# VectorE's w_ada chunks in halves around a linear chunk's two halves, in a two-block transformer kernel

## The chip, the cores and the metric

One NeuronCore of one Trainium2 chip runs the whole kernel. The metric is the device time of one execution in microseconds (us); the median of several runs counts. TensorE (PE in the profile) does the matrix products, VectorE (DVE) and ScalarE (ACT) work on elements, SyncE (SP) issues the DMA loads, GpSimd (POOL) does next to nothing here.

## The reference

Two blocks, batch 1, 256 tokens, width 2048, all in float32.

```
mod = silu(c) @ w_ada + b_ada                    # w_ada: 2048 x 12288; six parts of 2048
shift_a, scale_a, gate_a, shift_f, scale_f, gate_f = split(mod, 6)
h = rms_norm(x, g_attn_pre) * (1 + scale_a) + shift_a
proj = h @ w_in                                  # 5456 columns
mixed = concat(differential_attention(...), indexed_sparse_attention(...)) @ w_o
x = x + gate_a * rms_norm(mixed, g_attn_post)
h = rms_norm(x, g_ffn_pre) * (1 + scale_f) + shift_f
x = x + gate_f * rms_norm((silu(h @ w_gate) * (h @ w_up)) @ w_down, g_ffn_post)
x = second_block(x)                              # latent attention, a gated convolution; no w_ada
```

`silu(c) @ w_ada` is a vector times a matrix of 96 MB; the other products have 256 rows.

## The kernel before

**Chunks.** All weights pass through one ring of five slots (`raw`, `NRAW` = 5) of 1 MB: a chunk is 512 rows by up to 512 columns, held as 128 partitions by four row blocks. `chunk_plan` writes down the order of all chunks by hand in `PLAN`: linear chunks (`lin`) and, strewn between them, chunks of w_ada (`ada`, group g of 512 columns, quarter j of the rows). SyncE loads them in that order (`load_chunk`); the load of chunk c waits until chunk c - 5 has been used: for a w_ada chunk of VectorE's until `s_ada` has counted it, for a linear chunk until the wlo of its second half is written (`s_lo`).

**A linear chunk** is used in two halves (units) of two row blocks. ScalarE copies a half, rounded, to `whi` (L1046), VectorE writes the rest, `raw - whi`, to `wlo` (L1656), and TensorE makes twelve matmuls of it: activations hi times whi, hi times wlo, lo times whi (L579 to L581), for two blocks of 128 tokens. There are three slots of whi and wlo (`NHL`): whi of unit i waits for the matmuls of unit i - 3.

**A w_ada chunk** is used in one of two ways. The 32 chunks of groups 0 to 7 are done by TensorE (L533), all before 180 us. The other 64 (groups 8 to 23) are VectorE's: `ada_step` adds four row blocks, each scaled by an element of silu(c), to two accumulators (L1636, L1639), in turn even and odd; after quarter 3 it adds the two (L1648, `s_sum`). TensorE then sums over the partitions (`ada_take`, L514, L515 or L519), and VectorE's `mod` adds the bias or multiplies G by it (L1618, L1620) and frees the bank.

**The order of each engine's queue.** Every engine walks the same plan with a `Walk`. `UNITS` lists the halves of linear chunks and, as one entry each, the w_ada chunks, in the plan's order; `LIN` lists the linear halves alone. Before the matmuls of linear unit u, `chunk` calls `split_to`, which issues all that stands in `UNITS` up to linear unit u + 2 (`AHEAD` = 2). After the unit it calls `tick`, which lets each of up to three lanes of side work (attention heads in lane 0 and 1, the turning of operands) issue one step. So VectorE's queue is: the w_ada chunks that stand ahead of a linear chunk in the plan, wlo of its first half, a step of the lanes, wlo of its second half, a step of the lanes.

Between 176 us and 545 us (the last columns of w_in's first part, the rest of w_in, w_o) the plan has about one w_ada chunk of VectorE's ahead of each linear chunk, 48 in all, and two ahead of it at four places (before the w_in chunks that VectorE reaches at 206 and 315 us, and the first two chunks of w_o at 402 and 418 us). In the feed-forward part it has one ahead of every second linear chunk, 16 in all, until 880 us.

**When a group's sum is taken.** `split_to` notes in `sum_at` the linear unit at which the last quarter was issued; `can_take` lets the sum be taken two units later. It is taken by the lane of differential attention at fixed steps of it or, where lane 1 is empty, by `idle` at the next tick.

**G.** The gains of the post norm lie in `G`. The load of g_ffn_post into it (L2490) stands in SyncE's queue right behind the load of the chunk four places after the first one of w_gate's third column group; `mod` of group 20 multiplies G, in a tick at the end of w_up's second column group, ahead of the multiplies of `gt` (L2155) that end this w_up.

Of the kernel before, what the change touches and what calls it, by code (L numbers as in the profile page):

```python
# [46 lines left out]
ADA_ON_PE = (4, 0, 5, 1, 6, 2, 7, 3)  # L47
# [90 lines left out]

PLAN = chunk_plan()

UNITS = [(c, h) for c, item in enumerate(PLAN) for h in range(2 if item[0] == "lin" else 1)]
LIN = [u for u in UNITS if PLAN[u[0]][0] == "lin"]
LIN_NO = {u: i for i, u in enumerate(LIN)}
UNIT_AT = {u: i for i, u in enumerate(UNITS)}

ADA_NO = {c: i for i, c in enumerate(c for c, item in enumerate(PLAN) if item[0] == "ada" and item[1] not in ADA_ON_PE)}


def unit_after(w, k0, c0):
# [34 lines left out]
class Walk:  # L184
# [34 lines left out]
    def split_to(self, pos):  # L219
        while self.front <= pos and self.front < len(UNITS):  # L220
            c, h = UNITS[self.front]
            self.front += 1
            if c in ADA_NO and PLAN[c][2] == 0:
                self.groups.append(PLAN[c][1])
            if self.split and (c in ADA_NO or PLAN[c][0] == "lin"):
                self.split(c, h)
            if c in ADA_NO and PLAN[c][2] == 3:
                self.sum_at.append(self.unit)

    def can_take(self):  # L230
# [269 lines left out]
def tensor_program(m):  # L500
# [21 lines left out]
    def ada_products(c):  # L522


        while c < len(PLAN) and PLAN[c][0] == "ada" and c not in ADA_NO:
            _, g, j = PLAN[c]
# [507 lines left out]
def scalar_program(m):  # L1034
# [5 lines left out]
    def split(c, h):  # L1040
        if c in ADA_NO:
            return
        i, n = LIN_NO[c, h], PLAN[c][4]
        need.wait_ge(m.s_raw[c % NRAW], 16 * (c // NRAW + 1))
        need.wait_ge(m.s_mm, i - NHL + 1)
        act.activation(m.whi[:, i % NHL, :, 0:n], m.raw[:, c % NRAW, 2 * h:2 * h + 2, 0:n], ACT.Copy).then_inc(m.s_hi, 1)  # L1046
# [554 lines left out]
def vector_program(m):  # L1601
# [19 lines left out]
                              ALU.add).then_inc(m.freed[b], 1)  # L1621
        mod_at[g] = b, n

    def ada_step(c):

        _, g, j = PLAN[c]
        idx = len(k.groups) - 1
        if j == 0 and idx > 1:
            assert k.groups[idx - 2] in mod_at, (k.unit, k.groups)
        need.wait_ge(m.s_raw[c % NRAW], 16 * (c // NRAW + 1))  # L1630
        need.wait_ge(m.s_v, cs_at)
        for jj in range(4):
            kb = 4 * j + jj
            w, o, col = m.raw[:, c % NRAW, jj, :], m.acc[:, idx % 2, jj % 2, :], m.cs[:, kb:kb + 1]
            if kb < 2:
                ins = dve.tensor_scalar(o, w, col, None, ALU.mult)  # L1636
            else:
                need.wait_ge(*half[jj % 2])
                ins = dve.scalar_tensor_tensor(out=o, in0=w, scalar=col, in1=o, op0=ALU.mult, op1=ALU.add)  # L1639
            if jj < 3:  # L1640
                half[jj % 2] = m.s_v, v.up(ins)
        ins.then_inc(m.s_ada, 1)
        half[1] = m.s_ada, ADA_NO[c] + 1
        if j == 3:
            need.wait_ge(*half[0])
            need.wait_ge(*half[1])
            o = m.acc[:, idx % 2, 0, :]
            dve.tensor_tensor(o, o, m.acc[:, idx % 2, 1, :], ALU.add).then_inc(m.s_sum, 1)  # L1648

    def split(c, h):  # L1650
        if c in ADA_NO:
            ada_step(c)
            return
        i, n = LIN_NO[c, h], PLAN[c][4]
        need.wait_ge(m.s_hi, i + 1)
        dve.tensor_tensor(m.wlo[:, i % NHL, :, 0:n], m.raw[:, c % NRAW, 2 * h:2 * h + 2, 0:n],  # L1656
                          m.whi[:, i % NHL, :, 0:n].bitcast(F32), ALU.subtract).then_inc(m.s_lo, 1)

    def idle():
        mod(k.groups[k.take()], 6, k.use(6))  # L1660
        yield

    k = Walk(split)
    k.idle = idle

# [889 lines left out]
```

## Time and profile before

| | us |
|---|---|
| median of 3 runs (2413.04 to 2414.85) | 2414.76 |
| the profiled execution | 2414.19 |
| its span | 2412.9 |
| PE busy | 2294.3 (95%) |
| PE weight load busy | 1862.3 (77%) |
| DVE busy | 1398.7 (58%) |
| ACT busy | 1065.1 (44%) |
| wlo (L1656), 760 instructions | 910.0 |
| multiply-adds of w_ada (L1639), 224 instructions | 153.3 |
| whi (L1046), 760 instructions | 790.5 |

Matmuls are pipelined and their ends modelled, so a busy TensorE overlaps itself; the time from one start to the next is what counts. An idle time in brackets in a timeline is that of the engine just before the instruction, with what ended it. PEclk is the granted TensorE clock as a share of full speed.

### The profile page before, as it was taken

The page shows a single profiled execution, that of the slowest core. Times are in us where ns is not written, and L with a number is a line of the kernel's source. Part 1 is how long each engine was busy: PE and PEld are TensorE (multiplying, and loading weights), DVE is VectorE, ACT ScalarE, POOL GpSimd, SP SyncE. Part 2 cuts the span into 40 slices and gives each one's busy share as a digit, 9 for nine tenths or more (in the row PEclk, how much of TensorE's full clock was granted, in tenths as well). Part 3 has the DMA queues.
Part 4 walks back from the last instruction along what each step waited for, and adds up shares of the span by engine and source line. Part 5 has one row for each costly group of instructions (what it writes and reads, how often), then busy time and mean ns, then how long its engine had stood idle before and what let it go on. Part 6 is the DMA issues. An engine that isn't in the chain of part 4 may idle for free.

```text
span 2412.9 us, 26313 instructions
## 1 busy us (share of the span) xinstructions
PE 2294.3 (95%) x10768; PEld 1862.3 (77%) x10768; DVE 1398.7 (58%) x1903; ACT 1065.1 (44%) x1471; POOL 0.7 (0%) x5
## 2 busy tenths in 40 slices
PE   4999988898999999999998999999999999999998
PEld 2676767777788888888887878888888888888886
DVE  1459998786665464554555555454544554554554
ACT  2433444444344444434444555555444444444443
POOL 0000000000000000000000000000000000000000
PEclk8999999998999999999999999999999999999999
DMA  8988677593776575556554645454556555556553
GB/s 306 335 319 297 232 259 277 191 349 122 264 261 241 192 251 189 190 191 193 191 191 134 219 149 160 144 167 146 184 192 195 188 192 192 190 182 195 184 191 140
DMA packets 255455, 505.69 MB, mean 210 GB/s; under 512 B 9077, under 2 KB 19662, under 8 KB 254182
## 3 DMA queue, kind: packets, MB, share of 16 engines
q1 hardware_dynamic: 255334, 504.00, 62.0%
q8 instruction: 85, 1.39, 0.2%
q14 instruction: 36, 0.29, 0.0%
HBM read 499.77 MB, written 4.19 MB: 209 GB/s over the span
## 4 chain that ended last, share of the span: by engine, by line
PE 86%; DVE 7%; DMA 3%; ACT 2%; issue 1%; SPq 0%; DVEq 0%; ACTq 0%
PE bank L579 27%; PE bank L581 26%; PE bank L580 26%; DVE wlo L1656 2%; DVE acc L1639 2%; PE bank L595 2%; DMA raw<-in_w_in_dram 2%; PE bank L663 1%; ACT whi L1046 1%; DMA raw<-in_w_ada_dram 1%; PE bank L533 1%; PE bank L603 1%; DVE x L1708 0%; PE bank L686 0%; PE bank L666 0%
## 5 line engine op out<-in xcount | busy, mean ns | idle before, releaser
L1656 DVE TENSOR_TENSOR wlo<-raw,whi 128x1024 fp32r<-128x1024 f32 (+2 forms) x760 | 910.0, 1204 | 874.0 <-ACT whi L1046 873.6
L1046 ACT ACTIVATE whi<-raw 128x1024 fp32r<-128x1024 f32 (+2 forms) x760 | 790.5, 1044 | 1055.0 <-PE bank L581 971.8
L579 PE MATMUL bank<-whi,Ahi 128*128 128x512 f32 (+2 forms) x2304 | 914.0, 397 | 33.0 <-DVE wlo L1656 21.8
L580 PE MATMUL bank<-wlo,Ahi 128*128 128x512 f32 (+2 forms) x2304 | 897.8, 390 | 0.0
L581 PE MATMUL bank<-whi,Alo 128*128 128x512 f32 (+2 forms) x2304 | 897.5, 390 | 0.0
L579 PEld LDWEIGHTS bank<-whi,Ahi 128*128 128x128 f32 x2304 | 438.5, 190 | 136.1 <-DVE wlo L1656 32.8
L581 PEld LDWEIGHTS bank<-whi,Alo 128*128 128x128 f32 x2304 | 437.8, 190 | 90.8
L580 PEld LDWEIGHTS bank<-wlo,Ahi 128*128 128x128 f32 x2304 | 439.1, 191 | 83.8
L1639 DVE SCALAR_TENSOR_TENSOR acc<-raw,cs,acc 128x512 f32<-128x512 f32 x224 | 153.3, 744 | 0.0
L579 PE MATMUL bank<-whi,Fhi 128*128 128x512 f32 x352 | 137.7, 391 | 0.0
L581 PE MATMUL bank<-whi,Flo 128*128 128x512 f32 x352 | 137.0, 389 | 0.0
L580 PE MATMUL bank<-wlo,Fhi 128*128 128x512 f32 x352 | 137.0, 389 | 0.0
L579 PE MATMUL bank<-whi,Bhi 128*128 128x512 f32 x256 | 101.0, 395 | 0.0
L581 PE MATMUL bank<-whi,Blo 128*128 128x512 f32 x256 | 99.8, 390 | 0.0
L580 PE MATMUL bank<-wlo,Bhi 128*128 128x512 f32 x256 | 99.7, 390 | 0.0
L579 PEld LDWEIGHTS bank<-whi,Fhi 128*128 128x128 f32 x352 | 66.1, 188 | 14.4 <-issue 0.8
L581 PEld LDWEIGHTS bank<-whi,Flo 128*128 128x128 f32 x352 | 66.1, 188 | 13.8
L580 PEld LDWEIGHTS bank<-wlo,Fhi 128*128 128x128 f32 x352 | 66.1, 188 | 13.5
L581 PEld LDWEIGHTS bank<-whi,Blo 128*128 128x128 f32 x256 | 48.1, 188 | 10.3
L579 PEld LDWEIGHTS bank<-whi,Bhi 128*128 128x128 f32 x256 | 48.1, 188 | 9.8 <-issue 0.3
L580 PEld LDWEIGHTS bank<-wlo,Bhi 128*128 128x128 f32 x256 | 48.1, 188 | 9.6
L533 PE MATMUL bank<-raw,cs 128*32 128x512 f32 x256 | 35.4, 672 | 20.8 <-DMA raw<-in_w_ada_dram 20.8
(291 smaller groups left out, 1347.4 us busy)
## 6 DMA issues: line engine op xcount, KB each, us to landing
raw<-in_w_in_dram SPq DMA_DIRECT2D x156, 1024.0 KB, 5.0
raw<-in_w_ada_dram SPq DMA_DIRECT2D x96, 1024.0 KB, 5.4
raw<-in_w_gate_dram SPq DMA_DIRECT2D x44, 1024.0 KB, 5.1
raw<-in_w_up_dram SPq DMA_DIRECT2D x44, 1024.0 KB, 5.1
raw<-in_w_down_dram SPq DMA_DIRECT2D x44, 1024.0 KB, 5.0
raw<-in_w_o_dram SPq DMA_DIRECT2D x16, 1024.0 KB, 5.1
raw<-in_w_o_mla_dram SPq DMA_DIRECT2D x16, 1024.0 KB, 4.9
raw<-in_w_o_conv_dram SPq DMA_DIRECT2D x16, 1024.0 KB, 5.0
```

Source lines behind the costliest of these rows:

```text
L533: ins = pe.matmul(m.bank[b][32 * jj:32 * jj + 32, :], m.cs32[:, 4 * j + jj, :], m.raw[:, c % NRAW, jj, :], start=(j == 0), stop=(j == 3))
L579: pe.matmul(o, a_hi, w_hi, start=beg, stop=False)
L580: pe.matmul(o, a_hi, w_lo, start=False, stop=False)
L581: ins = pe.matmul(o, a_lo, w_hi, start=False, stop=fin)
L595: ins = pe.matmul(o, i, m.diag[:, tb, :], start=True, stop=True) if scaled else pe.transpose(o, i, m.ident)
L603: ins = pe.transpose(m.bank[b][:, tb * P:tb * P + P], src(tb), m.ident)
L663: pe.matmul(m.bank[ln.bank[mm]][:, PART[tb]], l, r, start=(i == 0), stop=False, skip_group_check=True)
L1046: act.activation(m.whi[:, i % NHL, :, 0:n], m.raw[:, c % NRAW, 2 * h:2 * h + 2, 0:n], ACT.Copy).then_inc(m.s_hi, 1)
L1639: ins = dve.scalar_tensor_tensor(out=o, in0=w, scalar=col, in1=o, op0=ALU.mult, op1=ALU.add)
L1656: dve.tensor_tensor(m.wlo[:, i % NHL, :, 0:n], m.raw[:, c % NRAW, 2 * h:2 * h + 2, 0:n], m.whi[:, i % NHL, :, 0:n].bitcast(F32), ALU.subtr ...
```

## The change

The list of units has two entries for each of VectorE's w_ada chunks (row blocks 0 and 1, and 2 and 3). The halves that stand ahead of a linear chunk are dealt out: the first half of them ahead of its first unit, the others between its two units. With one w_ada chunk that is one half ahead and one between; with two it is one chunk ahead and one between. `s_ada` counts at the end of the second half, where the final add of a group's two accumulators also stands, and `sum_at` is noted there. TensorE's w_ada chunks are no longer in the list; ScalarE and TensorE do nothing at VectorE's entries, as before. The order of the loads is as it was.

```
@@ module level
-UNITS = [(c, h) for c, item in enumerate(PLAN) for h in range(2 if item[0] == "lin" else 1)]
+def half_chunks():
+    units, side = [], []
+    for c, item in enumerate(PLAN):
+        if c in ADA_NO:
+            side += [(c, 0), (c, 1)]
+        elif item[0] == "lin":
+            n = len(side) // 2
+            units += side[:n] + [(c, 0)] + side[n:] + [(c, 1)]
+            side = []
+    assert not side
+    return units
+
+UNITS = half_chunks()
@@ Walk.split_to
-            if c in ADA_NO and PLAN[c][2] == 0:
+            if c in ADA_NO and PLAN[c][2] == h == 0:
                 self.groups.append(PLAN[c][1])
-            if self.split and (c in ADA_NO or PLAN[c][0] == "lin"):
+            if self.split:
                 self.split(c, h)
-            if c in ADA_NO and PLAN[c][2] == 3:
+            if c in ADA_NO and PLAN[c][2] == 3 and h == 1:
                 self.sum_at.append(self.unit)
@@ vector_program, ada_step
-    def ada_step(c):
+    def ada_step(c, h):
...
-        for jj in range(4):
+        for jj in (2 * h, 2 * h + 1):
...
+        if h == 0:
+            return
         ins.then_inc(m.s_ada, 1)
```

## Rows read from the trace of the kernel before

**Rows 1.** The page's chain of work that ended last, by engine (shares of the span).

```profile
PE 86%; DVE 7%; DMA 3%; ACT 2%; issue 1%; SPq 0%; DVEq 0%; ACTq 0%
```

**Rows 2.** Windows: length, then busy us (instructions) by engine, PEclk, DMA share, GB/s.

```profile
176.00:212.00 36.00, 30.24 (x133) 22.69 (x131) 35.56 (x61) 12.65 (x14) 0.00 (x0) 1.00 0.84 286
283.00:329.00 46.00, 36.54 (x149) 27.27 (x148) 43.78 (x111) 18.62 (x40) 0.00 (x0) 0.89 0.63 208
329.00:397.00 68.00, 66.80 (x348) 54.34 (x349) 61.23 (x114) 33.73 (x73) 0.00 (x0) 1.00 0.85 295
```

**Rows 3.** Waits, 170 to 560 us: total, times, longest, us.

```profile
DVE wlo L1656 <- ACT whi L1046: 14.7, 12, 2.4
```

**Rows 4.** Timeline of TensorE: start, us, what; in brackets its idle time before.

```profile
212.02 0.79 PE L579 MATMUL bank<-whi,Ahi 128*128 128x512 f32 x1 [3.66 <-DVE wlo L1656]
...
329.13 0.50 PE L579 MATMUL bank<-whi,Ahi 128*128 128x512 f32 x1 [0.88 <-DVE wlo L1656]
...
348.19 0.35 PE L686 MATMUL bank<-P,ET_a 128*128 128x128 f32 x1 [0.71 <-DVE ET_a L1925]
...
409.42 0.50 PE L663 MATMUL bank<-qT_b 64*128 64x256 f32 x2 [3.65 <-DVE modT L1620]
...
470.36 0.35 PE L686 MATMUL bank<-P,ET_a 128*128 128x128 f32 x1 [1.90 <-DVE ET_a L1925]
...
500.53 0.50 PE L579 MATMUL bank<-whi,Ahi 128*128 128x512 f32 x1 [0.45 <-DVE wlo L1656]
...
658.95 0.66 PE L595 MATMUL bank<-const,gt 128*128 128x128 f32 x2 [2.05 <-DVE gt L2155]
```

**Rows 5.** Timeline of VectorE, 393 to 410 us.

```profile
393.53 1.23 DVE L1656 TENSOR_TENSOR wlo<-raw,whi 128x1024 fp32r<-128x1024 f32 x1 [1.68 <-ACT whi L1046]
...
401.98 5.38 DVE L1639 SCALAR_TENSOR_TENSOR acc<-raw,cs,acc 128x512 f32<-128x512 f32 x8
...
408.07 1.22 DVE L1656 TENSOR_TENSOR wlo<-raw,whi 128x1024 fp32r<-128x1024 f32 x1
409.21 0.15 DVE L1620 TENSOR_TENSOR modT<-bank,bT 128x4 f32<-128x4 f32 x1
```

**Rows 6.** Timeline of VectorE, 464 to 471 us.

```profile
465.88 2.73 DVE L1639 SCALAR_TENSOR_TENSOR acc<-raw,cs,acc 128x512 f32<-128x512 f32 x4
468.53 1.22 DVE L1656 TENSOR_TENSOR wlo<-raw,whi 128x1024 fp32r<-128x1024 f32 x1
```

**Rows 7.** Timeline of VectorE, 242 to 284 us.

```profile
242.16 0.48 DVE L2043 SCALAR_TENSOR_TENSOR Ex_b<-Ex_b,sm_b 128x256 f32<-128x256 f32 x1
...
283.48 0.18 DVE L1889 RECIPROCAL sm_b<-sm_b 128x4 f32<-128x4 f32 x1 [0.35 <-ACT Ex_b L1175]
```

**Rows 8.** Timeline of TensorE, 243 to 244 us.

```profile
243.03 0.27 PE L676 MATMUL bank<-const,Ex_b 128*128 128x128 f32 x1
```

**Rows 9.** Windows of 2.8 us, right behind the stall at 212 and later.

```profile
212.10:214.90 2.80, 2.80 (x7) 2.22 (x8) 2.80 (x5) 0.00 (x0) 0.00 (x0) 0.50 1.04 395
218.10:220.90 2.80, 2.80 (x15) 2.29 (x14) 2.77 (x10) 0.75 (x2) 0.00 (x0) 1.00 0.99 330
```

**Rows 10.** Timeline of all engines, 649 to 657 us.

```profile
649.34 0.50 SPq L2490 DMA_DIRECT2D G<-in_g_ffn_post_dram  x1
...
656.96 0.69 DVE L1618 TENSOR_TENSOR G<-G,bank 128x512 f32<-128x512 f32 x1 [5.00 <-DMA G<-in_g_ffn_post_dram]
```

**Rows 11.** Timeline of all engines, 499 to 510 us.

```profile
499.37 0.37 SPq L2453 DMA_DIRECT2D raw<-in_w_o_dram  x1
...
506.36 1.06 ACT L1046 ACTIVATE whi<-raw 128x1024 fp32r<-128x1024 f32 x1 [1.72 <-PE bank L581]
...
509.89 1.22 DVE L1656 TENSOR_TENSOR wlo<-raw,whi 128x1024 fp32r<-128x1024 f32 x1
```

**Rows 12.** DMA issues, 176 to 560 us: times, KB each, median us to landing.

```profile
raw<-in_w_o_dram SPq DMA_DIRECT2D x16, 1024.0 KB, 5.1
raw<-in_w_gate_dram SPq DMA_DIRECT2D x4, 1024.0 KB, 6.7
```

More of the change, by code:

```diff
@@ L139 @@
 PLAN = chunk_plan()
-UNITS = [(c, h) for c, item in enumerate(PLAN) for h in range(2 if item[0] == "lin" else 1)]
+ADA_NO = {c: i for i, c in enumerate(c for c, item in enumerate(PLAN) if item[0] == "ada" and item[1] not in ADA_ON_PE)}
+def half_chunks():
[10 more added lines that the diff above has]
+UNITS = half_chunks()
 LIN = [u for u in UNITS if PLAN[u[0]][0] == "lin"]
@@ L144 @@
 UNIT_AT = {u: i for i, u in enumerate(UNITS)}
-ADA_NO = {c: i for i, c in enumerate(c for c, item in enumerate(PLAN) if item[0] == "ada" and item[1] not in ADA_ON_PE)}
 def unit_after(w, k0, c0):
@@ L1622, in mod @@
         mod_at[g] = b, n
-    def ada_step(c):
+    def ada_step(c, h):
         _, g, j = PLAN[c]
         idx = len(k.groups) - 1
-        if j == 0 and idx > 1:
+        if j == h == 0 and idx > 1:
             assert k.groups[idx - 2] in mod_at, (k.unit, k.groups)
@@ L1651, in split @@
         if c in ADA_NO:
-            ada_step(c)
+            ada_step(c, h)
             return
```

## The prediction

> **What bounds the kernel now.** I read first the page's chain of work that ended last. It is TensorE for 86% and VectorE for 7% [rows 1]. So most of what VectorE does costs nothing, and the question is where its 7% (some 170 us) lies. The same chain in order of time, by stretches, puts nearly all that this change can touch between 176 us and 545 us, plus one place near 650 us; before 176 us TensorE takes the w_ada chunks itself, and after 880 us there are none.
>
> Second, the windows [rows 2]. From 176 to 212 us VectorE is busy 35.56 of 36 us and TensorE only 30.24; from 283 to 329 us it is 43.78 of 46 against 36.54. There VectorE is the bound. From 329 to 397 us TensorE is (66.80 of 68). The kernel swings between the two, and only the handovers matter: an order inside VectorE's queue that leaves its total alone gains nothing inside a VectorE-bound stretch, only where TensorE waits for an early item of the queue and VectorE has slack later.
>
> Third, whether there is such slack. In 170 to 560 us VectorE's wlo waits 14.7 us for ScalarE's whi, 12 times [rows 3], which waits for TensorE to free a whi slot: VectorE is then its full two halves ahead. So each microsecond won for TensorE before such a place is kept.
>
> Fourth, TensorE's idle places one by one [rows 4]: 3.66 us at 212, 0.88 at 329, 0.71 at 348, 3.65 at 409, 1.90 at 470, 0.45 at 500 (0.44 more at 524), 2.05 at 659. The rest of its idle time in these stretches waits for work that the change doesn't move ahead: softmax and top-k steps behind both halves, the four Alo steps of w_o, and 10.3 us for the norm before the feed-forward part.
>
> **What the change does, part by part.** Write A for half a w_ada chunk, L0 and L1 for the wlo of a linear chunk's halves, J0 and J1 for what the lanes put behind each. Before, VectorE's order is A A L0 J0 L1 J1; after, A L0 J0 A L1 J1. With two w_ada chunks ahead it was A A A A L0, and is A A L0 J0 A A L1. No instruction is added or removed. Half a chunk is two instructions, 5.38 us for eight [rows 5], so 1.35 us. L0 and J0 therefore come 1.35 us earlier (2.7 at doubled places, and 0.6 to 0.7 more where the group's final add stood in front); L1 and J1 stay where they were.
>
> The price of switching kinds: four multiply-adds from 465.88 take 2.73 us, to 468.61, and the next wlo starts at 468.53 [rows 6], so a change of kind hides 0.08 us just as a run of one kind does. I take nothing. The other bound is 0.08 for each of two new boundaries in 48 chunks, 7.7 us of VectorE time, of which what lies in VectorE-bound stretches (about a quarter) would cost 2 us. The Trainium skill ("VectorE: DVE Perf Modes", The DRAIN you can't avoid) says that the next operation doesn't start until the pipe is empty, which speaks for that bound; by the rows here it starts 0.08 us before, and the sum by the skill's rule would be up to 2 us less gain.
>
> *At 212 us.* TensorE waits 3.66 us for the L0 behind a doubled chunk [rows 4]. L0 comes 2.7 us sooner, and I reckon that TensorE's next half starts about 4 us sooner, as the clock doesn't fall (below). But VectorE's total to 283 us is the same, and on the way its results are due again: its softmax step ends at 242.64 [rows 7] and TensorE's transposes of it start at 243.03 [rows 8]; that step is a J0 and gains 1.35, so TensorE keeps a lead of 0.39 + 1.35, some 1.7 us. At 283.48 VectorE's softmax job is a J0 that waits for ScalarE [rows 7]; now an A stands behind it that stood before it, so the VectorE-bound stretch that follows starts 1.35 us worse. Net 0.4 us (bounds 0 and 2).
>
> *At 329 us.* The stall of 0.88 before an L0 goes: together 1.3. *At 348 us* TensorE waits 0.71 us for a J0 (an ET_a copy); that goes: 2.0.
>
> *At 409 us* TensorE waits 3.65 us for bank 6's release by VectorE's modT add at 409.21, a J0 behind eight multiply-adds from 401.98, the group's add (0.7 us) and L0 at 408.07 [rows 4, 5]. After, it stands behind four and L0: 401.98 + 2.7 + 1.15 = 405.8. TensorE was done at 405.77, so with its own 2.0 us it could be ready at 403.8; VectorE, which has 1.68 us of slack at 393 [rows 5] and starts this run 2 us earlier too, delivers at 403.9 to 404.1. The scores start at about 404.1 instead of 409.42: together 5.3. The clock: after such a gap TensorE's granted clock is the lower of its two levels, 1.2 GHz (0.50), for some 3 us, in which it runs half as many matmuls as at 2.4 GHz [rows 9]; without it about 0.8 us comes back, 6.1. The following Alo steps have the same work ahead of them in both orders.
>
> *At 470 us* TensorE waits 1.90 us for the ET_a copy at 469.66, a J0 behind four multiply-adds and L0 [rows 4, 6]. It comes 1.35 us sooner, and with half a microsecond of gap left perhaps half of the 1.2 us of slow clock comes back (0.6): together 8.1. *At 500 and 524 us* the stalls of 0.45 and 0.44 before an L0 go: 9.0.
>
> *Near 650 us.* SP issues the load of G at 649.34, right behind the load that waited for the last w_ada chunk of group 20; VectorE's multiply of G waits 5.00 us for its landing (656.96), the gt multiplies stand behind it, and TensorE's transposes of gt wait 2.05 us for those [rows 4, 10]. The last A is now behind L0, so the slot and the load of G come 1.4 us later. But the group's sum is noted one half later, so TensorE takes it after the next half, and VectorE's multiply of G moves behind the gt multiplies. These then wait only for TensorE. The later landing (658.4) holds up one wlo that TensorE needs at about 663. So 2.05 us goes, and about 1.2 of slow clock behind it: together 12.2.
>
> *What it costs at SP.* A w_ada chunk's slot comes free one wlo (and J0) later, 1.13 us or more, and the linear chunk five places on is loaded that much later. In w_o's last columns a load is issued at 499.37 and its whi starts at 506.36, 7.0 us on [rows 11]; w_o's loads land in 5.1 us (median) [rows 12]. So 1.9 us of slack becomes 0.8, and whi is itself 3.5 us ahead of its wlo at 509.89 [rows 11]. Nothing, by these rows.
>
> Sum: the profiled execution took 2414.2 us (span 2412.9 and 1.3 around it). Less 12.2 it is 2402.0; the median of the runs is 0.6 above the profiled one: 2402.6. Its own range, by the bounds above (0 to 2 at 212, 0 or 2 for boundaries, 0 to 2.6 for the clock), is 2399 to 2407.
>
> **The rivals.**
> 1. *The jobs eat it.* VectorE's queue is in order; a J0 that must wait for ScalarE or TensorE now has an A behind it, as at 283. If the earlier L0s make most J0s gated, L1 comes up to 1.35 us late and VectorE-bound stretches keep their length. For it: the 212 and 283 places. Against it: only one of the waits of VectorE's jobs that I found stands between L0 and L1 ahead of a VectorE-bound stretch. Then 329, 348, 212 and half of 409 give nothing, and the gain is 3 to 7 us: 2408 to 2412.
> 2. *G's multiply stays in front of gt* (if the group's sum were taken where it was). The later landing then lengthens that stall by 1.4 us instead of ending it: 12.2 less 3.3 less 1.4 leaves 7.5, 2407. Against it: the count that lets TensorE take a sum runs from the half in which its last part is issued.
> 3. *Late slots, slower.* Two slots are now freed within about 2.6 us of each other, so loads come in pairs. w_gate's first loads, which are issued in a burst, land in 6.7 us [rows 12]. If the loads of a linear chunk land in 7.5 us or more, whi is late by over 1.4 us, and wlo, whose own slack falls from 4.2 to about 1.0, by the same less that; at 9 us each of the some fifteen pairs of w_o loses 1.5 us or more, in all over 20 us: 2410 to 2425. It decides from about 0.8 us lost per pair. Against it: single loads behind one other land in 5 to 5.8.
> 4. *Nothing to be seen.* TensorE's lead is lost at the norm before the feed-forward part or by VectorE's total: 2412 to 2416.
>
> Chances: forecast 0.62, rival 1 0.14, rival 2 0.09, rival 3 0.07 (slower 0.05, else same), rival 4 0.08. A measurement of this kernel can tell about 0.2%, 4.8 us, from no change. Faster by more: 0.62 + 0.09 + half of rival 1 (0.07) = 0.78, and 0.02 of late slots that only dent the gain, 0.80; same 0.15; slower 0.05. The range 2398 to 2411 leaves out rivals 3 and 4 and a little of the first.
>
> **What would show it.** In the new trace TensorE's stalls at 329, 348, 500 and 524 are gone, that at 409 is under 1 us and that at 470 about 0.5; the end of w_o's last chunk (541.5) is about 9 us earlier; no matmul waits for gt near 650, and VectorE's G multiply stands behind gt. VectorE's busy time stays at 1399 us. Wrong would be: new idle time of TensorE before an L1, new waits of whi for DMA in w_o, or a VectorE idle before a J0 with an A behind it in more places than the one at 283.

## The result, and the profile after

The changed kernel takes 2402.89 us (median of 4 runs, 2401.63 to 2403.83), the kernel before, beside it on the same chip, 2414.81 us (4 runs, 2413.04 to 2415.31): a ratio of 0.9954, 95% interval 0.9942 to 0.9966, so 8 to 14 us less. 2402.6 was forecast. The order of the steps was right too, but not every size, and one cost that I had put at nothing because it would not occur did occur and was hidden.

The page after has a span of 2402.5 us (2412.9 before). Its chain by engine answers to [rows 1], and the two rows under it are wlo and the multiply-adds of w_ada:

```profile
PE 86%; DVE 7%; ACT 3%; DMA 2%; issue 1%; SPq 0%; DVEq 0%; ACTq 0%
...
L1674 DVE TENSOR_TENSOR wlo<-raw,whi 128x1024 fp32r<-128x1024 f32 (+2 forms) x760 | 912.8, 1205 | 871.9 <-ACT whi L1062 870.2
...
L1655 DVE SCALAR_TENSOR_TENSOR acc<-raw,cs,acc 128x512 f32<-128x512 f32 x224 | 157.2, 745 | 0.1
```

The same instructions as before; VectorE is busy 1400.4 us (1398.7 before). The shares alone would not tell that anything has changed: 10 us are 0.4% of the span.

The windows that answer to [rows 2], each 2.70 us later, since the profiled execution after came to its first VectorE chunk of w_ada at 180.43 us and that of before at 177.73:

```profile
178.70:214.70 36.00, 32.99 (x147) 25.16 (x147) 35.57 (x61) 12.55 (x15) 0.00 (x0) 1.00 0.85 291
285.70:331.70 46.00, 36.30 (x148) 26.77 (x147) 44.23 (x109) 17.24 (x36) 0.00 (x0) 0.89 0.59 205
331.70:399.70 68.00, 66.69 (x350) 54.18 (x349) 62.16 (x115) 33.93 (x74) 0.00 (x0) 1.00 0.83 295
```

VectorE is about as full as before in the first two (35.57 us for 35.56, 44.23 for 43.78); TensorE gets 2.75 us more in the first and nothing in the second. These are the two VectorE-bound stretches, and VectorE's total has hardly moved in them.

TensorE's idle places, as in [rows 4] (the number in brackets is the idle time before):

```profile
211.49 0.50 PE L595 MATMUL bank<-whi,Ahi 128*128 128x512 f32 x1 [0.87 <-DVE wlo L1674]
...
292.40 0.50 PE L595 MATMUL bank<-whi,Ahi 128*128 128x512 f32 x1 [0.76 <-DVE wlo L1674]
...
317.41 0.38 PE L692 MATMUL bank<-const,Ex_b 128*128 128x128 f32 x1 [4.01 <-DVE Ex_b L2061]
...
368.39 0.63 PE L619 MATMUL bank<-const,P 128*128 128x128 f32 x4 [0.95 <-DVE modT L1636]
...
407.90 0.70 PE L679 MATMUL bank<-qT_b 64*128 64x256 f32 x4 [0.21 <-DVE modT L1636]
...
466.56 0.46 PE L702 MATMUL bank<-P,ET_a 128*128 128x128 f32 x2 [0.60 <-DVE ET_a L1943]
```

The stall of 3.65 us has become 0.21, that of 1.90 has become 0.60, and those of 0.88, 0.71, 0.45, 0.44 and 2.05 have no counterpart. In the stretches that VectorE doesn't bound one is new: 0.95 at 368.39, behind a modT add that stands behind L1, to which the change gives nothing. In the two VectorE-bound stretches the idle time is dealt out anew: 3.66 at 212 has become 0.87, 0.51 and 1.21 (at 211, 216 and 228) and 1.39 before a take of a sum at 205; before it was 2.59, 2.08 and 3.54 at 297, 307 and 315, and now it is 0.76, 0.82, 0.96, 3.14 and 4.01 at 292, 298, 302, 308 and 317. Those at 216, 292 and 302 stand before an L1; in the kernel before, no idle time of over 0.3 us from 176 to 560 us waits for the wlo of an L1.

The VectorE rows behind the 0.21, to be read against [rows 5]:

```profile
401.44 1.41 DVE L1655 SCALAR_TENSOR_TENSOR acc<-raw,cs,acc 128x512 f32<-128x512 f32 x2
402.77 1.22 DVE L1674 TENSOR_TENSOR wlo<-raw,whi 128x1024 fp32r<-128x1024 f32 x1
403.90 2.74 DVE L1655 SCALAR_TENSOR_TENSOR acc<-raw,cs,acc 128x512 f32<-128x512 f32 x4
406.55 1.22 DVE L1674 TENSOR_TENSOR wlo<-raw,whi 128x1024 fp32r<-128x1024 f32 x1
407.69 0.16 DVE L1636 TENSOR_TENSOR modT<-bank,bT 128x4 f32<-128x4 f32 x1
```

Between the wlo at 402.77 and that at 406.55, the L0, stand four multiply-adds and not eight; the other four follow the modT add. The rows also settle the price of a change of kind: from the start of two multiply-adds to that of the next wlo it is 1.33 us (401.44 to 402.77), of four 2.65 (403.90 to 406.55), so two changes of kind for each pair in place of two for each four add nothing.

Near 650 us, all engines, against [rows 10]:

```profile
643.83 0.51 SPq L2508 DMA_DIRECT2D G<-in_g_ffn_post_dram  x1
...
645.24 1.28 DVE L2173 TENSOR_TENSOR gt<-gt,bank 128x512 f32<-128x512 f32 x2
...
649.66 0.66 PE L611 MATMUL bank<-const,gt 128*128 128x128 f32 x4
...
651.07 0.69 DVE L1634 TENSOR_TENSOR G<-G,bank 128x512 f32<-128x512 f32 x1 [3.42 <-DMA G<-in_g_ffn_post_dram]
```

The multiply of G still waits for its landing, 3.42 us, but behind the gt multiplies, and TensorE's transposes of gt wait for nothing.

**Time by stretches.** The table is put together from the timelines of all thirteen kernels profiled: the length of each stretch, from VectorE's first multiply of w_ada on. "to 283", "to 341" and "to 450" end at a transpose of TensorE that waits for ScalarE's softmax, "to 418" at the stall of some 2.5 us before an Alo step, "norm 1" at the 10.3 us stall for the norm before the feed-forward part, "gt 1" and "gt 3" at the first transposes of the first and third column group of gt, "norm 2" at the 4.92 us stall for a norm of the second block, "end" at the end of the span. The numbers in the names are those of before.

```
kernel           to 283   to 341   to 418   to 450   norm 1     gt 1     gt 3   norm 2      end      sum
before           105.70    57.43    77.75    31.07   102.17    58.26    97.06   603.06  1102.67  2235.17
after            104.28    57.80    73.10    30.98    98.21    58.36    93.05   602.92  1103.37  2222.07
wo_only          104.22    58.15    73.12    31.08    98.16    58.49    95.03   603.05  1104.34  2225.64
doubled_only     105.69    57.47    72.84    29.50   100.63    56.67    95.08   603.06  1103.97  2224.91
single_only      105.14    58.56    79.28    31.07    98.17    56.64    93.05   602.92  1103.35  2228.18
ffn_only         105.71    57.44    77.86    31.06   100.59    56.65    93.05   602.92  1104.71  2229.99
g20_late         105.70    57.45    78.68    31.07   100.55    56.68    93.16   603.06  1103.16  2229.51
g_early          105.74    57.50    77.83    31.07   102.22    58.50    93.27   603.06  1102.97  2232.16
sum_early        106.81    58.41    73.15    31.07    99.55    56.65    98.19   603.05  1103.01  2229.89
all_between      103.13    60.24    77.46    29.50    99.59    58.58    93.02   602.91  1103.58  2228.01
after_g_early    104.26    58.16    73.11    31.05    98.17    58.53    93.05   602.92  1103.45  2222.70
c75_whole        104.23    57.26    73.15    31.04    98.21    58.71    93.05   602.92  1106.01  2224.58
half_loads       104.24    58.27    73.09    31.07    98.16    58.59    93.05   602.92  1103.51  2222.90
```

Many stretches repeat within 0.1 us between kernels of the same order, which no median does (the kernel before ran from 2407.7 to 2420.8 us over all its runs). Each row is one execution, though, and where TensorE restarts behind a stall its granted clock differs from one execution to the next, so some stretches take one of several lengths for the same order: "to 341" (57.80 in the changed kernel, 58.15 to 58.27 in three kernels with its order there), "to 418" (77.75 to 77.86 with the order of before, and 78.68 in `g20_late`), "to 450" (31.0 to 31.1, and 29.50 in two), "norm 1" (100.6 or 102.2 with the order of before), "gt 1" (56.7 or 58.5). "gt 1" and "end" (1102.7 to 1106.0) say nothing of the change. The start ahead of the table, 176.2 to 180.4 us, varies too. From before to after the stretches give 1.42, -0.37, 4.65, 0.09, 3.96, -0.10, 4.01, 0.14 and -0.70: together 13.1.

### The profile page after: what moved, and what is told of

Its sections match the earlier page's. It is cut to its first block, busy times and chain, and to the rows that moved or that the text cites. A ratio compares the mean times of both kernels' runs of the same rounds, so it can differ in the third digit from the quotient of the medians.

```text
span 2402.5 us, 26312 instructions
## 1 busy us (share of the span) xinstructions
PE 2288.5 (95%) x10768; PEld 1858.3 (77%) x10768; DVE 1400.4 (58%) x1903; ACT 1065.3 (44%) x1471; POOL 0.7 (0%) x5
## 3 DMA queue, kind: packets, MB, share of 16 engines
q8 instruction: 85, 1.39, 0.2%
## 4 chain that ended last, share of the span: by engine, by line
PE 86%; DVE 7%; ACT 3%; DMA 2%; issue 1%; SPq 0%; DVEq 0%; ACTq 0%
PE bank L595 27%; PE bank L597 26%; PE bank L596 26%; DVE wlo L1674 2%; PE bank L611 2%; DMA raw<-in_w_in_dram 2%; DVE acc L1655 1%; PE bank L679 1%; ACT whi L1062 1%; DMA raw<-in_w_ada_dram 1%; PE bank L549 1%; PE bank L619 1%; DVE x L1726 0%; PE bank L702 0%; PE bank L531 0%
## 5 line engine op out<-in xcount | busy, mean ns | idle before, releaser
L597 PEld LDWEIGHTS bank<-whi,Flo 128*128 128x128 f32 x352 | 66.1, 188 | 13.9
L597 PEld LDWEIGHTS bank<-whi,Blo 128*128 128x128 f32 x256 | 48.1, 188 | 10.3
```

The lines of the kernel that those rows point to most:

```text
L597: ins = pe.matmul(o, a_lo, w_hi, start=False, stop=fin)
```

## The experiments

Eleven kernels. The edit is against the changed kernel where nothing else is said, and in `half_chunks` where no function is named. "Before" had medians of 2413.25 beside the first four, 2413.51 beside the next four, and 2414.9 beside the last three.

**Which part of the plan gives it.** `wo_only` deals out the halves of groups 8 to 19 alone, `ffn_only` those of groups 20 to 23 (the feed-forward part).

```
-            n = len(side) // 2
+            n = len(side) // 2 if side and PLAN[side[0][0]][1] < 20 else len(side)    # wo_only
+            n = len(side) // 2 if side and PLAN[side[0][0]][1] >= 20 else len(side)   # ffn_only
```

> The new order only for groups 8 to 19 (between 176 and 545 us), the feed-forward part's w_ada chunks whole as before. My theory: the gain up to the end of w_o stays (9 to 9.7 us) and the stall of the gt transposes at about 650 us comes back at its old size, 2.05 us with 1.2 us of slow clock behind it: 2405.8 (2404.5 to 2407). If the feed-forward half of the change gave nothing, 2403.

> The new order only for groups 20 to 23, in the feed-forward part; all before 545 us as in the kernel before. My theory: only the stall of 2.05 us at 659 and the slow clock behind it go, 3.3 us: 2411.5 (2410.5 to 2412.5). If that gain came from w_o's end reaching it earlier, no change: 2414.8.

Measured: `wo_only` 2405.72, ratio 0.9965 (0.9951 to 0.9978); `ffn_only` 2410.73, 0.9992 (0.9983 to 1.0001). The table says it more sharply than the medians: `wo_only` has the changed kernel's lengths up to norm 1 (within 0.4), `ffn_only` those of before (a shorter norm 1 stretch apart, which is the clock's; see below) and the changed kernel's in "gt 3". In this the parts do not hang on each other. The expected stall of 2.05 us with its slow clock did not come back whole in `wo_only`, though: TensorE waits 1.58 us for gt, the clock behind it stays at 1.00, and "gt 3" is 95.03 and not 97.06. The load of G took 7.17 us from its issue to VectorE's multiply there, and 7.62 in the kernel before, which is nearly the difference of the stalls. The medians alone would not show `ffn_only` to be faster (its interval reaches 1.0001).

**What ends the stall near 650.** Three kernels. `g20_late` is the kernel before with the sum of group 20 taken one unit later, in `split_to`; `g_early` is the kernel before with the load of G six chunk loads earlier (the expectations call it eight; four linear chunks and two of w_ada lie between); `after_g_early` is that on the changed kernel.

```
-                self.sum_at.append(self.unit)
+                self.sum_at.append(self.unit + (PLAN[c][1] == 20))          # g20_late
-    at_gain2 = chunk_ahead(unit_after("w_up", 12, 512) - 1)
+    at_gain2 = chunk_ahead(unit_after("w_gate", 12, 512) - 1)               # g_early, after_g_early
```

> The kernel before, all w_ada chunks whole, with one edit: the sum of group 20 may be taken one linear half later. My theory is that the gain near 650 us is due to the place of VectorE's multiply of G in its queue (behind the gt multiplies) and not to the halves: 3.3 us faster, 2411.5, G's load still issued at about 649.3 and its landing still waited for by VectorE's multiply, but no matmul waits for gt. Rival, that the halves themselves free VectorE there: 2414.8.

> The kernel before with one edit: G's load (g_ffn_post) is issued eight chunks earlier, so that it has landed long before VectorE multiplies it. If the late landing is the whole cause of the stall of 2.05 us at 659, it goes and the time is 2411.5; if the multiply of G ahead of gt also had to wait for TensorE's taking of the sum, some of the stall would stay: 2412 to 2414.

> The changed kernel with G's load issued eight chunks earlier. By my theory the G step is already hidden behind gt in the changed kernel, so nothing changes: 2402.9 (2402 to 2403.8). If VectorE's wait of 3.4 us for G still cost anything behind it, 2400 to 2402.

Measured: 2410.20, ratio 0.9986 (0.9977 to 0.9995); 2412.30, 0.9995 (0.9986 to 1.0005); 2403.79, 0.9962 (0.9948 to 0.9976). In "gt 3" the first two take 93.16 and 93.27 where before takes 97.06 and the changed kernel 93.05. So the whole gain of this place is had by moving one multiply of VectorE, with no half anywhere. These are stretches of one execution each; of the medians that of `g_early` is not clear of noise. `g20_late`, all engines:

```profile
648.58 1.29 DVE L2155 TENSOR_TENSOR gt<-gt,bank 128x512 f32<-128x512 f32 x2
...
653.11 0.66 PE L595 MATMUL bank<-const,gt 128*128 128x128 f32 x4
...
653.25 0.69 DVE L1618 TENSOR_TENSOR G<-G,bank 128x512 f32<-128x512 f32 x1 [2.25 <-PE bank L515]
```

The gt multiplies run 4.7 us ahead of the multiply of G; in the changed kernel they are 5.8 ahead. One part of the expectation failed: the multiply of G waits here for TensorE's sum (2.25 us) and not for the load. `g_early` gets there the other way: G has landed, its multiply stays in front and waits 2.04 us for TensorE's sum, and no matmul waits for gt. On the changed kernel the earlier load gives nothing (2222.70 against 2222.07 in the sum), as it must if there the place is already free.

**The same on the whole plan: the sum back where it was.** `sum_early` notes a group's sum at the unit of before, in `split_to`, though its last half now stands behind the L0.

```
-                self.sum_at.append(self.unit)
+                nxt = next(i for i, u in enumerate(LIN) if u[0] > c)
+                self.sum_at.append(min(self.unit, nxt - AHEAD))
```

> The changed kernel with the group's sum noted where it was before (two halves after the linear unit ahead of which the plan has the last quarter), so that only the halves' order is left of the change. My theory: the new stall of 0.95 us at 368 us (a modT add one step late) goes, but VectorE's multiply of G stands ahead of gt again with its load issued later, so that the gt transposes wait some 3.4 us: 2403 - 1 + 3.3 + 1.4 = 2406.7 (2405 to 2408). If the place of the taking doesn't matter: 2402.9.

Measured: 2410.21, ratio 0.9990 (0.9981 to 0.9999), 3.5 us more than I had expected (2406.7). "gt 3" is 98.19, 5.1 more than in the changed kernel and 1.1 more than before: rival 2, with a price of 1.1 us where it had said 1.4. All engines near 650, and TensorE near 205:

```profile
653.72 0.69 DVE L1635 TENSOR_TENSOR G<-G,bank 128x512 f32<-128x512 f32 x1 [5.81 <-DMA G<-in_g_ffn_post_dram]
...
654.33 1.28 DVE L2174 TENSOR_TENSOR gt<-gt,bank 128x512 f32<-128x512 f32 x2
...
655.70 1.09 PE L612 MATMUL bank<-const,gt 128*128 128x128 f32 x4 [3.18 <-DVE gt L2174]
```

```profile
204.55 1.50 PE L531 MATMUL bank<-acc,const 128*128 128x512 f32 x2 [4.79 <-issue]
```

What I had missed is the second row. The take of a sum is an item of TensorE's queue, and if it stays where it was while the sum itself is made later, TensorE stands before it: 4.79 us, put down to issue because the profile shows no releaser (1.39 at the same take in the changed kernel). The placing of this wait is read from the order of the queue, not from a named releaser; at 508.98 us the same kernel has a take with one, 0.76 us for the add of the two accumulators (DVE acc L1667). The other half of the expectation failed: the stall at 368 did not go (0.94 us, at 371.21), so it doesn't hang on when the sum is taken. Moving `sum_at` with the last half is thus a part of the change that it can't do without, not only at group 20.

**Doubled places and single ones.** `doubled_only` deals out halves only at the four places with two chunks ahead, `single_only` only where there is one.

```
-            n = len(side) // 2
+            n = len(side) // 2 if len(side) > 2 else len(side)      # doubled_only
+            n = len(side) // 2 if len(side) == 2 else len(side)     # single_only
```

> The new order only at the four places with two w_ada chunks ahead of a linear chunk (one stays ahead, one goes between); single chunks stay whole. My theory: the lead won at 212 us (about 1.4 to 1.7 us) is kept at 283 us, since no half stands behind the gated softmax step there, the stalls at 329, 348, 470, 500, 524 and 659 stay, and that at 409 us shrinks by 2.7 us: 4 to 5 us faster, 2410. If the single halves carry the gain, 2413 to 2415.

> Halves only where one w_ada chunk stands ahead of a linear chunk; at the four places with two ahead both stay whole and ahead. My theory (the 409 us stall and its slow clock hang on the doubled place alone, the rest on the single ones): the stall of 3.65 us before the scores near 409 us is back, and the stretch from 341 to 418 us takes 77 to 77.8 us (changed 73.10, before 77.75); the stretch from 450 us to the norm before the feed-forward part stays near 98.2, and the feed-forward part keeps its 3.3 us; about 5 us slower than the changed kernel, 2407 to 2408. If the gains of the single places need the doubled ones ahead of them (rival), it is 2410 or more.

Measured: `doubled_only` 2406.07, ratio 0.9973 (0.9960 to 0.9986), 4 us less than my theory had said; `single_only` 2410.97, 0.9988 (0.9975 to 1.0001), 3 to 4 us more than my theory had said. The profiled execution of `doubled_only` shows where time that I hadn't forecast can come from: it is 1.6 us shorter than before in "to 450", 1.5 in "norm 1", 1.6 in "gt 1" and 2.0 in "gt 3", at places where the stalls are still there (the gt one 1.65 us) and no slow clock stands behind them (see the last section). How much of the miss in the median that is, these runs don't show. TensorE in `doubled_only`, and then in `single_only`:

```profile
209.62 0.50 PE L595 MATMUL bank<-whi,Ahi 128*128 128x512 f32 x1 [1.01 <-DVE wlo L1674]
...
218.39 0.50 PE L595 MATMUL bank<-whi,Ahi 128*128 128x512 f32 x1 [1.70 <-DVE wlo L1674]
...
227.89 0.50 PE L595 MATMUL bank<-whi,Ahi 128*128 128x512 f32 x1 [1.97 <-DVE wlo L1674]
```

```profile
213.93 0.72 PE L595 MATMUL bank<-whi,Ahi 128*128 128x512 f32 x1 [3.52 <-DVE wlo L1674]
...
412.75 1.23 PE L679 MATMUL bank<-qT_b 64*128 64x256 f32 x4 [3.65 <-DVE modT L1636]
```

With the doubled places alone the stall of 3.66 at 212 is cut to 1.01, and 1.70 and 1.97 come up behind it: the stretch to 283 is bound by VectorE's total and stays at 105.69. "To 418" is all the doubled places' (72.84; without them the 3.65 is back, and the stretch is 79.28), and the stretch to norm 1 is all the single ones' (98.17). The parts do depend on each other here, which I had not foreseen. The single ones alone give 0.56 to 283 and lose 1.13 to 341, so they stand 0.57 behind before at 341; the doubled ones alone change nothing; both together are 1.05 ahead. And "to 418" of `single_only` is 1.5 longer than before with the same stall, of which 1.3 lies behind that stall (10.45 us from the scores to the end of the Alo stall, 9.19 before), where the granted clock is 0.50 for 6 us (before 0.56, then 0.88). Lengths like these come without any difference of order: `ffn_only` and `g_early`, with the order of before, take 9.30 and 9.29 there, and `g20_late` takes 10.17.

**More than half behind.** `all_between` puts the whole of what stood ahead between L0 and L1 (`n = 0`).

> The changed kernel with the w_ada chunks not in halves but whole, all of them behind the linear chunk's first half (L0 J0 A A L1; A A A A where there were two). First halves come another 1.35 us (2.7) earlier, second halves stay. By my theory TensorE has hardly a stall left that waits for a first half, so little more is won (the 0.6 at 470, parts of the small ones near 190 to 230 and 292 to 308), while a lane's step that waits now holds back a whole chunk: 2401 to 2406. If slots that come free later are the bound (late slots), it is clearly worse than the change: 2408 or more, with waits of whi for DMA growing beyond 41 us.

Measured: 2408.44, ratio 0.9979 (0.9969 to 0.9990); I had said 2401 to 2406. TensorE:

```profile
316.42 0.47 PE L692 MATMUL bank<-const,Ex_b 128*128 128x128 f32 x1 [7.25 <-DVE Ex_b L2061]
...
420.12 0.77 PE L595 MATMUL bank<-whi,Ahi 128*128 128x512 f32 x1 [4.21 <-DVE Alo L1712]
```

Against before it gains 2.57 to 283 and gives 2.81 back to 341: the wait for the last softmax product of VectorE, 4.01 in the changed kernel, is 7.25 here. Against the changed kernel it also takes 4.4 more to 418, where the eight multiply-adds now stand ahead of the Alo step. What is taken from ahead of one item is put ahead of the next; half and half is the better deal. The median is in the range that I had given to late slots (2408 or more), but the sign that went with it is missing: whi waits 32.2 us for DMA from 170 to 560 us, less than the 41.5 of the changed kernel. VectorE's own wait for whi is 20.2 us here against 13.9; whether that costs anything no run shows.

**The half behind a gated step.** In `c75_whole` the one chunk ahead of the L0 at 283 us stays whole and ahead.

```
-            n = len(side) // 2
+            n = len(side) // 2 if side != [(75, 0), (75, 1)] else 2
```

> This is the changed kernel, but the one w_ada chunk ahead of the linear chunk at whose first half VectorE waits for ScalarE's softmax at 283 us stays whole, so that no half of a chunk stands behind that gated step. My theory (a lane step that waits for ScalarE holds up the half behind it, and the VectorE-bound stretch after it starts that much worse): the stretch from 283 to 341 us, 57.80 us in the changed kernel and 57.43 in the kernel before, shrinks by 0.4 to 1.35 us, to 56.5 to 57.4; all other stretches are as in the changed kernel; median 2402 to 2403. If the held-up half costs nothing there (rival), the stretch stays at 57.7 to 57.9, or grows because the first half of that linear chunk comes 1.35 us later.

Measured: 2403.60, ratio 0.9954 (0.9937 to 0.9970). VectorE in the changed kernel, then in `c75_whole`:

```profile
280.54 1.41 DVE L1655 SCALAR_TENSOR_TENSOR acc<-raw,cs,acc 128x512 f32<-128x512 f32 x2
283.08 1.23 DVE L1674 TENSOR_TENSOR wlo<-raw,whi 128x1024 fp32r<-128x1024 f32 x1 [1.13 <-ACT whi L1062]
284.76 0.18 DVE L1907 RECIPROCAL sm_b<-sm_b 128x4 f32<-128x4 f32 x1 [0.45 <-ACT Ex_b L1191]
...
289.80 1.42 DVE L1655 SCALAR_TENSOR_TENSOR acc<-raw,cs,acc 128x512 f32<-128x512 f32 x2
```

```profile
278.19 2.73 DVE L1655 SCALAR_TENSOR_TENSOR acc<-raw,cs,acc 128x512 f32<-128x512 f32 x4
280.84 1.21 DVE L1674 TENSOR_TENSOR wlo<-raw,whi 128x1024 fp32r<-128x1024 f32 x1
282.40 0.18 DVE L1907 RECIPROCAL sm_b<-sm_b 128x4 f32<-128x4 f32 x1 [0.34 <-ACT Ex_b L1191]
```

With half a chunk ahead VectorE has too little to do until ScalarE is ready and idles 1.13 + 0.45 us; with the whole one it idles 0.34. Behind that it has no idle time up to TensorE's wait for the last softmax product, at 313.73 us here:

```profile
313.73 0.47 PE L692 MATMUL bank<-const,Ex_b 128*128 128x128 f32 x1 [4.92 <-DVE Ex_b L2061]
```

From the end of "to 283" to that matmul it is 31.38 us in `c75_whole` and 31.36 to 31.38 in the five kernels that have the chunk whole and ahead (before among them), 32.68 to 32.71 in the six with half of it behind, and 34.00 in `all_between`: 1.3 us for each half, the 1.35 of the prediction. Of this 0.5 to 1.0 is left at 341 (57.26 against 57.80 in the changed kernel and 58.15 to 58.27 in its three siblings with the same order); the rest was lost behind the wait, where the granted clock was 0.56 for 6 us here, 0.72 in the changed kernel and 0.64 in `wo_only`. This is rival 1's mechanism at its one place. In the median it is not to be seen, so I keep no version of this kernel as better than the changed one.

**Late slots.** In `half_loads` the loads of VectorE's w_ada chunks bring 256 of 512 columns; the other columns of w_ada are left out of the result (stale data is used).

```
@@ load_chunk
+        if c in ADA_NO:
+            n = 256
```

> The changed kernel, but the loads of VectorE's w_ada chunks bring only columns 0 to 255 of 512; the rest of the slot holds what was there, so the w_ada products are not the reference's. The instructions of all engines and their order stay; the bytes of these loads halve, and ScalarE's waits for late loads (41.5 us in 170 to 560 us in the changed kernel) should go to under 10. My theory (these waits are hidden, since ScalarE runs ahead of VectorE): all stretches from 176 us on as in the changed kernel within 0.3 us, the last columns of w_o within 1.6 us for its clock, median 2402 to 2404, if the start before 176 us is alike. Rival (late slots cost a part of the gain): the w_o stretches get shorter by 1 us or more, and the median is under 2401.

Measured: 2401.74, ratio 0.9947 (0.9932 to 0.9962). ScalarE's waits for loads from 170 to 560 us, in the changed kernel and then here (total, times, longest):

```profile
ACT whi L1062 <- DMA raw<-in_w_in_dram: 23.0, 7, 7.3
...
ACT whi L1062 <- DMA raw<-in_w_o_dram: 18.5, 6, 4.2
...
DVE wlo L1674 <- ACT whi L1062: 13.9, 14, 2.2
```

```profile
ACT whi L1062 <- DMA raw<-in_w_in_dram: 22.7, 7, 6.9
...
DVE wlo L1674 <- ACT whi L1062: 12.2, 12, 2.2
...
ACT whi L1062 <- DMA raw<-in_w_o_dram: 3.9, 2, 2.1
```

Before it was 5.1 us in all. The median is 0.3 us under my range and 0.7 over the rival's. My expectation that the waits would fall under 10 us failed (26.6): those in w_in did not go, so they hardly come from bytes in flight; that they come from when the slots are freed is argued, not shown, and so this run can't tell what they cost. Those in w_o did go, from 18.5 to 3.9, and still "norm 1" is 98.16 against 98.21. The other stretches are the changed kernel's too, the one to 341 being that of its siblings. What ScalarE waits in w_o costs nothing.

## Why the prediction was right, and where it was not

**The signs.** What was to show it came: the stalls at 329, 348, 500 and 524 are gone, that at 409 is 0.21, that at 470 is 0.60, and the norm's stall ends 9.75 us earlier, counted from VectorE's first multiply of w_ada. But all three signs of being wrong came too. TensorE idles before three L1s (0.51, 0.76 and 0.96 us), whi waits 18.5 us for DMA in w_o (before not at all), and VectorE idles before two J0s with an A behind them, at 284.76 and 380.34 us (0.45 each). The first lies in stretches that VectorE bounds and cost no more than is said below, the second was hidden, and the second place of the third lies where VectorE isn't the bound. They were chosen too wide to refute anything.

**Before 341 us** I had reckoned 1.3 and measured 1.05. The lead of 1.7 carried to 283 is 1.42, but only halves at both kinds of place carry it. The start 1.35 worse behind the gated step was named rightly: `c75_whole` puts it at 1.3 up to 317 us, of which 0.5 to 1.0 is left at 341.

**348 us.** The 0.71 was won and lost again: 0.95 appears at 368.39, since VectorE is full there and the modT add stands behind L1. `doubled_only`, which keeps a stall of 0.73 at 348, has none at 368 and gets to 418 in 72.84 against 73.10. I should have looked for the next due result of VectorE behind 348, as I did behind 212.

**409 us.** Forecast 3.3 and 0.8 of clock, together with the 0.7 above 4.8; measured 4.65 for the stretch. Inside it the parts differ: counted from the first multiply the scores start at 227.47 and not 231.69, so 4.2 us earlier and not 5.3, and from there to the end of the Alo stall it takes 7.71 us instead of 9.19, which is 1.5 where I had put 0.8 for the clock (granted 0.56 and then 0.88 before, 1.00 in the changed kernel; with the order of before this part was also 9.29, 9.30 and 10.17). Two errors met, so that the sum came out is luck. That the doubled place alone gives it was right.

**450 us to norm 1.** Forecast 1.36 + 0.6 + 0.9 = 2.9, measured 3.96. The mechanism holds (0.60 left at 466.56, none at the two L0s, all of it from single places); the term mis-sized is the slow clock. Kernels with the order of before take 100.6 or 102.2 here; against the first the gain is 2.4, against the second 4.0, and the profiled execution of before was of the second kind.

**Near 650 us.** Forecast 3.3, of which 1.2 clock; "gt 3" shows 4.01. From the first to the second column group's transposes it is 2.34 (48.84 to 46.50 us), from there to the third's 1.67 (48.22 to 46.55), and that second part is clock (windows below). That the sum's later place does it was right: with the sum at its old place the stall is 3.18, with only that one sum moved it is gone.

**At SP** the step failed, without a price. I had turned 1.9 us of slack into 0.8 and concluded "Nothing, by these rows", and that is not what happened. Loads did come in pairs, as rival 3 said. SP and ScalarE of the changed kernel, against [rows 11]:

```profile
500.34 0.37 SPq L2471 DMA_DIRECT2D raw<-in_w_o_dram  x1
...
501.47 0.37 SPq L2471 DMA_DIRECT2D raw<-in_w_ada_dram  x1
...
502.54 2.01 ACT L1062 ACTIVATE whi<-raw 128x1024 fp32r<-128x1024 f32 x2 [4.20 <-DMA raw<-in_w_o_dram]
```

and its DMA issues from 176 to 560 us, against [rows 12]:

```profile
raw<-in_w_o_dram SPq DMA_DIRECT2D x16, 1024.0 KB, 6.7
```

Landing rose from 5.1 to 6.7 us, under the 7.5 from which I had reckoned a price, and whi waited up to 4.2 us, as none had in w_o before. It cost nothing, since VectorE's wait for whi did not grow (13.9 us against 14.7): ScalarE's lead absorbed it. The time was right for the second of the two reasons that the step gave, not for the first.

**The sum.** 12.2 forecast; 11.9 in the medians, 13.1 in the stretches. The 1.2 between them is less than the start and the two stretches that vary by themselves move a run, and both lie in the interval of 8 to 14. My lower bound was added up wrongly: from the bounds named there the range is 2401 to 2408 and not 2399 to 2407; and the 0.02 that the chances give to late slots as still faster stands against the "else same" before it. Neither changes the outcome. No rival held: 1 is one place, 2 needs the sum at its old place, 3 stayed under its threshold by the median (6.7; one of the 16 loads took 7.56), 4 is refuted by norm 1.

## What to carry to other kernels

In an in-order queue, ask of each item who waits for it, and put work that nobody awaits half ahead of it and half behind; moving all of it behind only moves the stall. Before crediting a won stall, find the next result of the same engine that will be due, and whether the engine is full until then. A count that lets another engine take a result has to move with the result.

## What the runs showed of the hardware

How much clock a stall costs is not fixed by its length alone. Windows behind the stall at gt, in the kernel before (2.05 us of idle time) and in `wo_only` (1.58), same instructions; the third number from the end is the granted clock, 1.00 being 2.4 GHz and 0.50 being 1.2:

```profile
658.95:661.95 3.00, 3.00 (x9) 2.54 (x10) 3.00 (x4) 0.60 (x1) 0.00 (x0) 0.50 0.02 7
```

```profile
650.54:653.54 3.00, 3.00 (x15) 2.54 (x16) 3.00 (x4) 0.60 (x1) 0.00 (x0) 1.00 0.03 8
```

Nine matmuls against fifteen; "gt 3" is 97.06 and 95.03, so a stall 0.47 us longer cost 2.0. And behind the stall of 1.90 us near 470, in two kernels with the same order up to there, before and then `g20_late`:

```profile
470.36:473.36 3.00, 3.00 (x15) 2.81 (x16) 1.76 (x3) 0.00 (x0) 0.00 (x0) 0.64 1.01 369
473.36:476.36 3.00, 3.00 (x12) 2.36 (x12) 0.00 (x0) 0.00 (x0) 0.00 (x0) 0.79 0.83 321
```

```profile
470.08:473.08 3.00, 3.00 (x19) 2.73 (x20) 1.76 (x3) 0.00 (x0) 0.00 (x0) 1.00 0.96 360
473.08:476.08 3.00, 3.00 (x19) 2.56 (x18) 0.58 (x1) 1.21 (x3) 0.00 (x0) 1.00 0.81 313
```

Same stall, same work, one with a fall of the clock and one without: 1.6 us, the two values of "norm 1". The two values of "gt 1" behind the 10.3 us stall (56.7 and 58.5) are alike, and so are those of "to 450": behind 2.46 us of idle time before the second Alo step the changed kernel was granted 0.74 for 6 us (28 matmuls, 30.98 us), behind 2.44 `doubled_only` was granted 1.00 (36 matmuls, 29.50). So a stall of about 2 us is worth its length or some 1.6 us more, and one profiled execution can't say which. By the Trainium skill ("TensorE: Matmul & The Clock Gate", What's actually happening) the number of slow matmuls at a kernel's start varies from run to run of one kernel; these rows, behind stalls in its middle, agree.

Two multiply-adds and a change of kind cost half of what four and a change of kind cost (1.33 and 2.65 us, the rows of VectorE above), so nothing of the bound of 2 us that I had kept for the boundaries was paid. The Trainium skill ("VectorE: DVE Perf Modes", The DRAIN you can't avoid) has the next operation wait until the pipe is empty, and adds that one that is not held starts earlier, which I had left out. Whichever applies, it is already in each operation's own time here, of one kind or mixed.
